# Two-block transformer on one core: filler and convolution taps of the differential stage dealt by what each part costs

## The chip, the cores and the metric

The program runs on one core of one Trainium2 chip. The metric is the device time of one execution in microseconds. The kernel before took 3533.0 us in the median of three runs (3526.06 to 3537.19). TensorE (PE) multiplies matrices, VectorE (DVE) and ScalarE (ACT) work on rows of 128 partitions, GpSimd (POOL) likewise, SyncE (SP) issues the transfers.

## What is computed

Two transformer blocks, one behind the other, over 1024 rows of 1024 columns, all in fp32. The change lies in the second block, in its differential attention and its depthwise convolution:

```
h = rms_norm(x, attn_norm_w)
q, k, v, u, g = split(h @ w_in)                 # 1024, 1024, 1024, 2048, 2048 columns
q, k = rms_norm(q), rms_norm(k)                 # over 64 columns, 8 heads x 2 maps
p = softmax(q1 k1' * scale + bias, causal) - lam * softmax(q2 k2' * scale + bias, causal)
a = rms_norm(p @ v) ...                         # per head, over 128 columns
c = conv31(u_a * sigmoid(u_b))                  # causal, depthwise, 31 taps, 1024 channels
x = x + (g_a * (a @ w_proj_attn) + g_b * (silu(layer_norm(c)) @ w_proj_conv)) @ w_out
x = x + (silu(h2 @ w_gate) * (h2 @ w_up)) @ w_down
```

## The kernel before

fp32 products are made of three passes: each operand is split into a rounded high part and a remainder (`_hi`, `_lo`), and hi x hi, lo x hi and hi x lo are added up in PSUM. ScalarE rounds a tile of weights (`ring.round`, line 171), GpSimd subtracts (`ring.subtract`, line 179), through a ring of two slots; SyncE loads them.

The stage is `differential_and_conv`. Its attention runs in 64 steps: head h = s // 8, query block b = s % 8 of 128 rows, with (b + 1) x 128 keys. A step has three parts, x = 0, 1, 2; all engines walk the same list of steps and parts, each in its own queue, and wait on semaphores. In step s:

- TensorE: `score(s)` for both maps into `sc` (line 2471), then the parts. In each part it does its share of the *filler*: the projections of the next head's q, k, b, a, v tiles and of gate tiles G, 48 matmuls of 512 columns a tile in two halves of 24 (line 197). In part 0 of every odd step also `values` for a pair of earlier steps (line 2492), and in parts 0 and 2 `turn_t`, the transposes of the probabilities of step s - 1 into the one `bank` (line 341). `turn_t` waits for `mixed` (GpSimd) and for `t_low` of the block before it; `values` waits for the `t_low` of its own blocks.
- VectorE: `top(s)` adds the bias and takes the negated maximum (lines 2340, 2344); then in each part the first share of its convolution taps, in part 0 `weights` (2349, 2351), in parts 0 and 2 `low_t` (2358), the remainder of the turned block; then what the part has of `feed_conv` (2293), `low_v`, `normalise`, `low_q`, `low_k`; then the second share of the taps. A tap (2272) multiplies 128 x 1024 of the padded input by one weight per channel and adds to `acc`.
- ScalarE: `expose(s)`, both exponentials (2162), needs `top(s)`; then in each part, in this order: a square of a norm (2119), `take` of the projected halves that end in this part, each second half with the rounding of the weights two tiles on and, for b, with a table load, the sigmoid and a table load (2101 to 2104); `round_t` in parts 0 and 2 (2178); `weigh` in part 0 (2170); `copy_out`, `round_v`, `invert` (2126, 2129), `round_q`, `round_k`.
- GpSimd: weight subtractions, and in part 0 `mix(s)` (2056), which adds the two weighted maps.

Which part of a head has the extra work of a norm is set by constants: V_TURN = 4, Q_SQUARE = 5, O_SQUARE = 6, K_SQUARE = 8 (a part is numbered 3b + x, 0 to 23). The square is taken at that part, the sum of squares and the division one part later (q: in the same part), the rounding of k two parts later.

The filler was dealt over the steps by fixed weights (13, 13, 13, 13, 12, 12, 11, 11) and evenly over the three parts. The 31 taps of a head (13 of head 0 come before the loop) were dealt over the parts between the end of this head's `feed_conv` and two parts before the next one, so that TAP = 1.45 us a tap plus an estimate of VectorE's other work in each part follows an estimate of TensorE's (`pe_load`, `dve_load`).

Of the kernel before, what the change touches and what calls it, by code (L numbers as in the profile page):

```python
# [1851 lines left out]
def differential_and_conv(nc, ring, w_in, h_hi, h_lo, bias_rows, lam, ones, eps, qk_gain, subln, conv_w, conv_b,  # L1852
# [6 lines left out]
    with ExitStack() as stack:  # L1859
# [81 lines left out]
        def pe_load(at):  # L1941

            s, x = divmod(at, PARTS)
            b = s % QB
            lo, hi = part(s, x)
            return 0.231 * (hi - lo) + (0.24 * (b + 1) if x == 0 else 0.44) + (0.72 * (b + 1) if x == 0 and b % 2 else 0)

        def dve_load(at):

            s, x = divmod(at, PARTS)  # L1950
            b = s % QB
            load = {V_TURN: 1.4, Q_SQUARE: 1.3, Q_SQUARE + 1: 2.7, O_SQUARE + 1: 1.6, K_SQUARE + 1: 1.3,
                    K_SQUARE + 2: 2.6}.get(b * PARTS + x, 0)
# [301 lines left out]
        def _(dve):  # L2255
# [619 lines left out]
```

## Time and profile before

| | |
|---|---|
| median of three runs | 3533.0 us |
| the profiled execution | 3531.41 us, its span 3529.6 us |
| mean granted clock of TensorE | 0.919 |
| busy: PE, DVE, ACT, POOL | 3006.8, 1612.5, 1256.4, 711.3 us |
| taps (line 2272) | 240, 397.2 us, 1655 ns each |
| filler of the stage (line 197, d_pp) | 3 x 896 matmuls, 368.0, 368.8 and 366.0 us |

The stage's steps lie between about 1408 and 2286 us of the span. Head 0 starts at 1408 on TensorE, and the five heads after it take some 110 us each up to head 4; heads 5 and 6 have seven tiles of filler instead of six. Busy time of matmuls counts their overlapping ends: their pitch is shorter than their mean duration (0.233 us against some 0.4).

### The profile page before, as it was taken

To read this page: it belongs to the slowest core of one execution; us is meant where nothing else is said; L and a number is where in the kernel's file an instruction comes from. 1 tells how busy PE (TensorE), PEld (TensorE's weight loads), DVE (VectorE), ACT (ScalarE), POOL (GpSimd) and SP (SyncE) were. 2 spreads that over 40 slices of the span, in tenths; PEclk is the share of its full clock that TensorE was granted. 3 is DMA by queue.
4 is the path that set the end of the run, shared out by engine and by line. 5 is a ranking of instruction groups with operands and counts; after the bars stand their busy time and mean duration, and the time that the engine had idled before them with its cause. 6 is when DMAs were issued, how large, how long until landed. Compare 5 with 4: busy or idle time off the path is not lost. (4 is left out here: it accounts for less than half of the span.)

```text
span 3529.6 us, 35907 instructions
## 1 busy us (share of the span) xinstructions
PE 3006.8 (85%) x13416; PEld 2422.7 (69%) x13416; DVE 1612.5 (46%) x1983; ACT 1256.4 (36%) x2003; POOL 711.3 (20%) x317
## 2 busy tenths in 40 slices
PE   6999998766668859989889899977686998998998
PEld 5787886555556747767767677754475787787786
DVE  3665651356654333777877787511432221111121
ACT  3555541344442143555555445432223111111110
POOL 2111111100002211323332233211312121121211
PEclk8999999888869979999999999988798999999999
DMA  4111222000004312121221112133230111111112
GB/s 111 38 54 48 66 67 59 18 8 7 9 0 146 111 66 63 48 61 38 62 60 50 55 51 75 69 137 107 95 125 18 48 48 42 42 48 42 42 48 72
DMA packets 232494, 207.77 MB, mean 59 GB/s; under 512 B 25224, under 2 KB 196776, under 8 KB 232360
## 3 DMA queue, kind: packets, MB, share of 16 engines
q1 hardware_dynamic: 231328, 204.40, 18.6%
q10 hardware_dynamic: 1032, 1.57, 0.3%
q8 instruction: 85, 1.39, 0.2%
q14 instruction: 49, 0.40, 0.0%
HBM read 156.13 MB, written 41.42 MB: 56 GB/s over the span
## 5 line engine op out<-in xcount | busy, mean ns | idle before, releaser
L179 POOL TENSOR_TENSOR w_lo<-w_raw,w_hi 128x1024 fp32r<-128x1024 f32 (+2 forms) x228 | 536.5, 2355 | 2214.7 <-ACT w_hi L171 2214.7
L171 ACT ACTIVATE w_hi<-w_raw 128x1024 fp32r<-128x1024 f32 (+2 forms) x228 | 223.7, 985 | 780.1 <-PE u_y_ps L1649 222.4
L2272 DVE SCALAR_TENSOR_TENSOR d_acc<-d_padded,vectors,d_acc 128x1024 f32<-128x1024 f32 x240 | 397.2, 1655 | 4.5
L197 PE MATMUL d_pp<-h_hi,w_hi 128*128 128x512 f32 x896 | 368.0, 411 | 12.2 <-PEq L67 5.2
L197 PE MATMUL d_pp<-h_hi,w_lo 128*128 128x512 f32 x896 | 368.8, 412 | 0.0
L197 PE MATMUL d_pp<-h_lo,w_hi 128*128 128x512 f32 x896 | 366.0, 408 | 0.0
L197 PE MATMUL s_pp<-h_hi,w_hi 128*128 128x512 f32 x512 | 206.8, 404 | 12.1 <-PEq L67 12.1
L197 PEld LDWEIGHTS d_pp<-h_hi,w_hi 128*128 128x128 f32 x896 | 175.1, 195 | 56.0 <-issue 18.0
L2056 POOL TENSOR_TENSOR d_probs<-d_probs 128x128 f32<-128x128 f32 (+3 forms) x64 | 123.5, 1930 | 410.4 <-ACT d_probs L2170 410.2
L197 PE MATMUL s_pp<-h_hi,w_lo 128*128 128x512 f32 x512 | 205.2, 401 | 0.0
L197 PE MATMUL s_pp<-h_lo,w_hi 128*128 128x512 f32 x512 | 204.2, 399 | 0.0
L197 PEld LDWEIGHTS d_pp<-h_lo,w_hi 128*128 128x128 f32 x896 | 174.3, 195 | 41.8 <-issue 2.6
L197 PEld LDWEIGHTS d_pp<-h_hi,w_lo 128*128 128x128 f32 x896 | 174.9, 195 | 39.8 <-issue 2.1
L2162 ACT ACTIVATE d_probs<-d_sc,d_stats 128x256 f32<-128x256 f32 (+7 forms) x128 | 94.3, 739 | 295.5 <-DVE d_stats L2344 295.0
L1649 PE MATMUL u_y_ps<-w_hi,ff_hi 128*128 128x512 f32 x352 | 140.7, 400 | 27.1 <-PEq L67 27.1
L1649 PE MATMUL u_y_ps<-w_hi,ff_lo 128*128 128x512 f32 x352 | 140.1, 398 | 0.0
L1649 PE MATMUL u_y_ps<-w_lo,ff_hi 128*128 128x512 f32 x352 | 139.5, 396 | 0.0
L1633 DVE TENSOR_TENSOR x_tok<-u_y_ps,x_tok 128x512 f32<-128x512 f32 x48 | 33.2, 691 | 232.4 <-PE u_y_ps L1649 232.4
L227 PE MATMUL t_g<-h_hi,w_hi 128*128 128x512 f32 x352 | 114.0, 406 | 15.2 <-DVEq L208 15.2
L197 PEld LDWEIGHTS s_pp<-h_hi,w_hi 128*128 128x128 f32 x512 | 97.3, 190 | 31.9 <-issue 12.4
L2680 DVE TENSOR_TENSOR t_t<-t_g,t_t 128x1024 f32<-128x1024 f32 x22 | 26.9, 1225 | 197.0 <-ACT t_t L2660 197.0
L2683 DVE TENSOR_TENSOR t_t<-t_u,t_t 128x1024 f32<-128x1024 f32 x22 | 26.9, 1224 | 195.8 <-PE t_u L227 195.8
(320 smaller groups left out, 6621.0 us busy)
## 6 DMA issues: line engine op xcount, KB each, us to landing
w_raw<-in_w_in SPq DMA_DIRECT2D x97, 512.0 KB, 4.0
w_raw<-in_w_gate_up SPq DMA_DIRECT2D x44, 512.0 KB, 3.9
w_raw<-in_w_down SPq DMA_DIRECT2D x22, 512.0 KB, 3.8
gates<-s_gate SPq DMA_DIRECT2D x16, 512.0 KB, 5.2
f_gate<-gates SPq DMA_DIRECT2D x16, 512.0 KB, 4.8
w_raw<-in_w_out SPq DMA_DIRECT2D x16, 512.0 KB, 4.1
w_raw<-in_w_proj SPq DMA_DIRECT2D x16, 512.0 KB, 5.0
x_tok_in<-in_x SPq DMA_DIRECT2D x8, 512.0 KB, 8.5
```

The source lines that it names most:

```text
L171: act.activation(self.hi[:, s, 0:chunks, :], self.raw[:, s, 0:chunks, :], ACT.Copy).then_inc(self.rounded[s], 1)
L179: pool.tensor_tensor(self.lo[:, s, 0:chunks, :], self.raw[:, s, 0:chunks, :], f32(self.hi[:, s, 0:chunks, :]), ALU.subtract).then_inc(self ...
L197: mm = pe.matmul(halves(ps)[h], w[:, k, :], x[:, k, h * HALF:(h + 1) * HALF], start=(k == 0 and r == 0), stop=(k == chunks - 1 and r == 2))
L227: mm = pe.matmul(halves(ps)[h], w[:, k, :], x[:, k, h * HALF:(h + 1) * HALF], start=(k == 0 and r < 2), stop=(k == chunks - 1 and r > 3))
L1633: dve.tensor_tensor(x, y_ps[b][:, :], x, ALU.add).then_inc(added, 1)
L1649: mm = pe.matmul(y_ps[b][:, :], y[:, k, b * P:(b + 1) * P], ww[:, i * HALF:(i + 1) * HALF], start=(k == 0 and r == 0), stop=(k == chunks - ...
L2056: pool.tensor_tensor(probs[:, s % 2, 0:n], probs[:, s % 2, 0:n], probs[:, 2, 0:n], ALU.add).then_inc(c["mixed"], 1)
L2162: act.activation(probs[:, slot, 0:n], sc[:, a, 0:n], ACT.Exp, bias=st[:, 1:2], accum_out=st[:, 2:3]).then_inc(c["prob"], 1)
L2272: dve.scalar_tensor_tensor(out=acc[:, :], in0=x, scalar=wt, in1=acc[:, :], op0=ALU.mult, op1=ALU.add).then_inc(c["taps"], 1)
L2680: dve.tensor_tensor(t[:, s, :], g_ps[s][:, :], t[:, s, :], ALU.mult).then_inc(silu[s], 1)
L2683: dve.tensor_tensor(t[:, s, :], u_ps[s][:, :], t[:, s, :], ALU.mult).then_inc(product[s], 1)
```

## The change

The first hunk deals the filler. `pe_work(h, at)` gives the microseconds that TensorE has in a part apart from filler; each part gets filler up to one common level of the head, so that filler (0.231 us a matmul) and the rest make equal sums, and a part above the level gets none. K_SQUARE moves from 8 to 9.

The second deals the taps. `dve_work(at)` gives VectorE's other microseconds in a part; each part of a head's room gets taps in proportion to what the level (all work of the room over its parts) leaves there, at least 0.2. TAP is 1.65. The room ends one part ahead of the next head's first `feed_conv` instead of two. The third halves a part's taps around the part's other work, and in part 0 of a step an odd tap comes first.

```diff
-        weight = [13, 13, 13, 13, 12, 12, 11, 11]
+        V_TURN, Q_SQUARE, O_SQUARE, K_SQUARE = 4, 5, 6, 9
+        def pe_work(h, at):
+            b, x = divmod(at, PARTS)
+            turned = min(4, b) if b else 4
+            work = {V_TURN: 0.9, Q_SQUARE: 1.7 * (h < LAST), O_SQUARE + 1: 1.7 * (h > 0),
+                    K_SQUARE + 1: 1.7 * (h < LAST)}.get(at, 0)
+            if x == 0:
+                work += 0.23 * (b + 1) + 0.11 * turned + {1: 2.9, 3: 0.7, 5: 1.5, 7: 2.2}.get(b, 0)
+            if x == 2:
+                work += 0.11 * (max(b - 4, 0) if b else 4)
+            return work
...
-            total = each[h] * SIX
-            at = [base + total * sum(weight[:b]) // sum(weight) for b in range(QB + 1)]
-            base += total
-            ends += [[lo + (hi - lo) * x // PARTS for x in range(PARTS + 1)] for lo, hi in zip(at, at[1:])]
+            fixed = [pe_work(h, at) for at in range(PARTS * QB)]
+            room = 0.231 * each[h] * SIX
...
+            total, share = 0.0, [max(level - f, 0) for f in fixed]
+            at = [base]
+            for x in share:
+                total += x
+                at.append(base + round(each[h] * SIX * total / sum(share)))
...
-        conv_end = [part_of[stream.index(("a", h)), 0] - 2 for h in range(1, HEADS)] + [PARTS * (STEPS - 1)]
+        conv_end = [part_of[stream.index(("a", h)), 0] - 1 for h in range(1, HEADS)] + [PARTS * (STEPS - 1) + 1]
-        TAP = 1.45
+        TAP = 1.65
...
+            n = CONV - (TAPS_FIRST if h == 0 else 0)
+            level = (sum(dve_work(at) for at in room) + TAP * n) / len(room)
+            free = [max(level - dve_work(at), 0.2) for at in room]
+            total, done = 0.0, 0
+            for at, x in zip(room, free):
+                total += x
+                upto = n if at == room[-1] else round(n * total / sum(free))
...
-            def taps(at, lo, hi):
+            def taps(at, first_half):
...
-                    for t in range(x + (y - x) * lo // 4, x + (y - x) * hi // 4):
+                    middle = x + (y - x + (at % PARTS == 0)) // 2
+                    for t in range(x, middle) if first_half else range(middle, y):
                         tap(h, t)
```

Worked out from these lines for head 2 (heads 1 to 4 are alike but for a tap), the steps separated by bars, the three parts of a step in a group:

```
filler before  12 13 13 | 12 13 13 | 12 13 13 | 12 13 13 | 12 12 12 | 11 12 12 | 10 11 11 | 11 11 11
filler after   14 16 15 |  1 13  9 | 12 10 16 |  8  9 17 |  9 17 16 |  2 17 16 |  7 17 15 |  0 17 15
taps before     0  3  2 |  1  2  1 |  0  0  2 |  2  0  3 |  0  0  0 |  0  2  2 |  0  1  2 |  4  2  2
taps after      0  3  2 |  1  1  2 |  0  2  2 |  1  1  1 |  1  2  0 |  0  0  2 |  0  3  2 |  0  2  3
```

The halves of a tile end, before, in parts 1 and 3 (q), 5 and 7 (k), 9 and 11 (b), 13 and 15 (a), 17 and 19 (v), 21 and 23 (G); after, in parts 1 and 4, 6 and 8, 10 and 12, 14 and 16, 17 and 19, 22 and 23. Taps of heads 0 to 7, before: 33, 31, 31, 31, 31, 34, 26, 18; after: 30, 31, 31, 31, 31, 35, 25, 21.

## Rows read from the trace of the kernel before

**Rows 1.** Busy by window: length, PE, PEld, DVE, ACT, POOL, then clock, DMA, GB/s
```profile
1628.00:1739.00 111.00, 98.78 (x453) 79.09 (x452) 85.23 (x95) 59.91 (x101) 32.67 (x14) 0.93 0.18 54
1964.00:2087.50 123.50, 111.21 (x504) 88.45 (x503) 96.76 (x98) 61.48 (x104) 35.11 (x15) 0.96 0.19 56
2087.50:2199.00 111.50, 107.58 (x505) 85.96 (x504) 77.69 (x92) 61.59 (x104) 34.43 (x15) 0.99 0.20 60
2193.00:2286.00 93.00, 90.89 (x450) 74.50 (x448) 61.80 (x75) 45.46 (x88) 24.80 (x14) 1.00 0.20 69
```

**Rows 2.** Waits of TensorE, 1628 to 1739 us: total, times, longest
```profile
PE d_bank L341 <- DVE d_t_lo L2358: 6.7, 1, 6.7
PE d_sc L2471 <- ACT d_probs L2162: 4.4, 1, 4.4
```

**Rows 3.** Windows as in rows 1, before and behind the longer hole
```profile
1585.30:1619.80 34.50, 34.50 (x176) 28.69 (x175) 27.92 (x29) 19.79 (x33) 13.19 (x5) 1.00 0.15 46
1622.90:1633.00 10.10, 5.63 (x16) 4.60 (x17) 9.33 (x13) 2.09 (x7) 2.92 (x2) 0.50 0.18 54
```

**Rows 4.** Waits of VectorE, 1628 to 1739 us: total, times, longest
```profile
DVE d_stats L2349 <- ACT d_probs L2162: 7.7, 6, 2.2
DVE d_t_lo L2358 <- ACT d_t_hi L2178: 6.1, 7, 1.4
DVE d_raw L2305 <- ACT d_probs L2129: 5.8, 2, 2.9
DVE d_o_sb L2305 <- ACT d_probs L2129: 2.6, 1, 2.6
DVE d_q L2311 <- ACT d_q L2136: 1.5, 1, 1.5
DVE d_sc L2340 <- PE d_sc L2471: 0.5, 1, 0.5
```

**Rows 5.** Timeline of VectorE, one head: start, duration, ..., [idle before <- releaser]
```profile
1616.24 10.52 DVE L2272 SCALAR_TENSOR_TENSOR d_acc<-d_padded,vectors,d_acc 128x1024 f32<-128x1024 f32 x5
...
1637.77 0.69 DVE L2358 TENSOR_TENSOR d_t_lo<-d_bank,d_t_hi 128x512 fp32r<-128x512 f32 x1 [1.35 <-ACT d_t_hi L2178]
...
1643.65 0.29 DVE L2358 TENSOR_TENSOR d_t_lo<-d_bank,d_t_hi 128x128 fp32r<-128x128 f32 x1 [1.35 <-ACT d_t_hi L2178]
...
1653.81 1.29 DVE L2305 SCALAR_TENSOR_TENSOR d_raw<-d_raw,vectors,d_probs 128x1024 f32<-128x1024 f32 x1 [2.90 <-ACT d_probs L2129]
...
1667.10 1.29 DVE L2305 SCALAR_TENSOR_TENSOR d_o_sb<-d_o_sb,d_gain,d_probs 128x1024 f32<-128x1024 f32 x1 [2.57 <-ACT d_probs L2129]
...
1678.21 1.28 DVE L2305 SCALAR_TENSOR_TENSOR d_raw<-d_raw,vectors,d_probs 128x1024 f32<-128x1024 f32 x1 [2.91 <-ACT d_probs L2129]
...
1692.94 0.17 DVE L2349 RECIPROCAL d_stats<-d_stats 128x2 f32<-128x2 f32 x1 [1.73 <-ACT d_probs L2162]
```

**Rows 6.** Timeline of ScalarE: a taken half with a weight rounding, two table loads
```profile
1641.75 0.59 ACT L2097 ACTIVATE d_raw<-d_pp 128x512 f32<-128x512 f32 x1
1642.22 1.05 ACT L171 ACTIVATE w_hi<-w_raw 128x1024 fp32r<-128x1024 f32 x1
...
1683.40 1.28 ACT L2101 ACT_TABLE_LOAD   x1
...
1685.78 1.28 ACT L2104 ACT_TABLE_LOAD   x1
```

**Rows 7.** Timeline of VectorE, head 5, step 3
```profile
2018.43 0.56 DVE L2358 TENSOR_TENSOR d_t_lo<-d_bank,d_t_hi 128x384 fp32r<-128x384 f32 x1 [4.94 <-ACT d_t_hi L2178]
```

**Rows 8.** Instructions of tile d_acc: ns shortest/median/longest
```profile
L2272 DVE SCALAR_TENSOR_TENSOR d_acc<-d_padded,vectors,d_acc x240: 1267/1285/3311, 1360.8 to 2284.4; 128x1024 f32<-128x1024 f32 x120
```

**Rows 9.** Costliest groups of the page: busy us, mean ns, idle before
```profile
L2272 DVE SCALAR_TENSOR_TENSOR d_acc<-d_padded,vectors,d_acc 128x1024 f32<-128x1024 f32 x240 | 397.2, 1655 | 4.5
```

**Rows 10.** Timeline of GpSimd: mixing of step 7, a weight subtraction
```profile
1617.76 3.32 POOL L2056 TENSOR_TENSOR d_probs<-d_probs 128x1024 f32<-128x1024 f32 x1 [6.15 <-ACT d_probs L2170]
...
1664.90 2.41 POOL L179 TENSOR_TENSOR w_lo<-w_raw,w_hi 128x1024 fp32r<-128x1024 f32 x1 [2.74 <-ACT w_hi L171]
```

More of the change, by code:

```diff
@@ L1907, in differential_and_conv @@
         TILES = len(stream)
-        weight = [13, 13, 13, 13, 12, 12, 11, 11]
+        V_TURN, Q_SQUARE, O_SQUARE, K_SQUARE = 4, 5, 6, 9
[9 more added lines that the diff above has]
+            return work
         ends, base = [], 0
         for h in range(HEADS):
-            total = each[h] * SIX
-            at = [base + total * sum(weight[:b]) // sum(weight) for b in range(QB + 1)]
-            base += total
-            ends += [[lo + (hi - lo) * x // PARTS for x in range(PARTS + 1)] for lo, hi in zip(at, at[1:])]
+            fixed = [pe_work(h, at) for at in range(PARTS * QB)]
+            room = 0.231 * each[h] * SIX
+            level = 0.0
+            for lower in sorted(fixed):
+                under = [f for f in fixed if f <= lower]
+                if sum(lower - f for f in under) <= room:
+                    level = (room + sum(under)) / len(under)
+            total, share = 0.0, [max(level - f, 0) for f in fixed]
[3 more added lines that the diff above has]
+                at.append(base + round(each[h] * SIX * total / sum(share)))
+            base += each[h] * SIX
+            ends += [at[PARTS * b:PARTS * (b + 1) + 1] for b in range(QB)]
         def part(s, x):
@@ L1936, in differential_and_conv, with dve_work @@
         conv_in_at = [-1] + [part_of[stream.index(("a", h)), 1] for h in range(1, HEADS)]
-        conv_end = [part_of[stream.index(("a", h)), 0] - 2 for h in range(1, HEADS)] + [PARTS * (STEPS - 1)]
+        conv_end = [part_of[stream.index(("a", h)), 0] - 1 for h in range(1, HEADS)] + [PARTS * (STEPS - 1) + 1]
         TAPS_FIRST = 13
-        TAP = 1.45
-        def pe_load(at):
+        TAP = 1.65
+        def dve_work(at):
             s, x = divmod(at, PARTS)
[L1944 to L1953, printed above, removed]
-            load += sum(0.7 for t, e in halves_in(s, x) if stream[t][0] == "a")
-            return load + (1.7 + 0.27 * (b + 1) + 0.4 if x == 0 else 0.5 if x == 2 and b > 4 else 0)
-        V_TURN, Q_SQUARE, O_SQUARE, K_SQUARE = 4, 5, 6, 8
+            h, b = divmod(s, QB)
+            load = {V_TURN: 1.4, Q_SQUARE: 1.3, Q_SQUARE + 1: 2.7, O_SQUARE + 1: 1.3, K_SQUARE + 1: 1.3,
+                    K_SQUARE + 2: 2.5}.get(at % (PARTS * QB), 0) * (h < LAST or at % (PARTS * QB) in (V_TURN, O_SQUARE + 1))
+            load += sum(0.7 for t, e in halves_in(s, x) if stream[t][0] == "a")
+            if x == 0:
+                load += 0.5 + (1.15 + 0.28 * (b + 1) if b < 4 else 0.8 + 0.285 * (b + 1))
+                load += 0.15 + 0.135 * (min(4, b) if b else 4)
+            if x == 2 and (b == 0 or b > 4):
+                load += 0.15 + 0.135 * (b - 4 if b else 4)
+            return load
         taps_in = {}
@@ L2378, in _ @@
                     at = b * PARTS + x
-                    taps(PARTS * s + x, 0, 2)
+                    taps(PARTS * s + x, True)
                     if s < STEPS and x == 0:
@@ L2400, in _ @@
                         low_k(h + 1)
-                    taps(PARTS * s + x, 2, 4)
+                    taps(PARTS * s + x, False)
             normalise("o", LAST)
```

6 lines of the change are left out of this document (removed).

## The prediction

> **What bounds the kernel now.** I read the busy windows first, one for each head of the stage. A head of the middle of the stage (heads 1 to 4) takes 111 us; in it TensorE (PE) is busy 98.8 us at a mean clock of 0.93, VectorE (DVE) 85.2 us [rows 1]. By these shares TensorE seems to set the pace and to have 12 us of holes. The waits say who made them: 6.7 us for VectorE's rounding remainder of the turned block (`low_t`) and 4.4 us for ScalarE's exponential [rows 2]. Each is one wait per head, and behind each the clock falls: behind the longer one 10.1 us pass at 0.50, that is at 1.2 GHz, while the 34.5 us of unbroken work before it ran at 1.00 [rows 3]. A mean of 0.93 over the head [rows 1] is 0.14 x 111 = 15.5 us at half clock, and costs half of it. So a head without the two would be 111 - 11.1 - 7.8 = about 92 us on TensorE.
>
> The waits of VectorE are the view that decides. In the same head they sum to 24.2 us: 7.7 + 6.1 + 5.8 + 2.6 + 1.5 + 0.5 [rows 4]. 85.2 + 24.2 = 109.4 of 111 us. VectorE is either working or standing for a short round trip over ScalarE, practically never for TensorE alone (0.5 us for the scores). So VectorE's in-order chain, work plus round trips, is the pace of heads 1 to 4, and TensorE's two large holes are only where that lag is collected. Over heads 0 to 5 the same holds (head 5: 96.8 us busy of 123.5); head 6 has 77.7 busy of 111.5 and head 7 61.8 of 93, where TensorE is 91 busy [rows 1]: there TensorE sets the pace, in head 7 wholly.
>
> **What that makes of the change.** Filler, scores and taps are the same in number. Levelling removes the places where the lag is collected, not the lag. A head gets shorter only by what VectorE's round trips lose, by taps that leave heads 0 to 5, and by what taps lose less to GpSimd. I count these for heads 1 to 4, part by part (part 3b + x is the x-th of step b, 0 to 23 in a head), on VectorE's queue.
>
> Round trips that shrink. (a) Part 3: a lone tap now stands between `top` and `weights` and covers that wait, one of the short ones among the six that make 7.7, about 0.6 [rows 4]; `q`'s second half is no longer taken in this part (with a weight rounding of 1.05), so the `low_t` wait of 1.35 goes: -2.0 [rows 5, 6]. (b) Part 2: the wait of 1.35 is for TensorE's transposes; a lagging VectorE doesn't meet it: -1.35 [rows 5]. (c) `normalise("q")` in part 5 waited 2.90; one tap now stands ahead of it: about -1.9 [rows 5]. (d) `normalise("o")` in part 7 waited 2.57; the taking of `k` with its weight rounding (0.59 + 1.05) leaves ScalarE's queue in front of it and one tap stands ahead: -2.6 [rows 5, 6]. (e) Part 12: the lone tap covers 1.2 of the 1.73 in front of `weights` [rows 5]. (f) The weight rounding leaves part 15, as in part 3: -1.4; the small rest of the `low_t` waits and the score wait, -1.3 [rows 4]. Sum -11.7.
>
> Round trips that grow. (g) The second half of `b` now ends in part 12, the first of a step. There ScalarE takes it before it rounds the turned block: 0.6 for the half, 1.05 for the next weights, then table, sigmoid and table, 3.66 from the first load's start to the second's end, 5.3 in all [rows 6], and `low_t` stands behind it on VectorE. In head 5 this order exists already and that one wait is 4.94 us [rows 7]. In heads 1 to 4 the old order has it in part 11, where nothing waits. +5.4. (h) Part 4 has one tap, behind `low_v`; in front stood two. After `weights` ScalarE has the scaling, 0.59, 1.05 and a half of v to do, some 3.1, VectorE only a `low_t` of 0.3: wait about +2.8 (estimate from [rows 6]). (i) Keys one part later: the square now stands behind `expose` of step 3 and in front of its rounding: `low_t` +0.9, and `normalise("k")` has 0.6 of `b` more before it: 2.91 becomes 3.7, +0.8 [rows 5, 6]. (j) Part 6: the taking of `k` stands before the rounding: +0.5. (k) Part 21 had four taps, two of them between `top` and `weights`; it has none, so the longest wait of that kind, 2.2, is met: +2.2 [rows 4]. In parts 15 and 18 nothing changes: no tap there before, none now. Sum +12.6.
>
> Net +0.9 us a head, nothing that the levelling was to win. Its bounds: if (c), (h) and (k) fall half as favourably, +6; if VectorE's lag hides (h) and (i), -5.
>
> **Taps beside GpSimd.** A tap alone takes 1.27, the longest 3.31 [rows 8], the mean is 1.655 [rows 9]. Five taps beside a mixing of 3.32 took 10.52, where alone they would be 6.35 [rows 5, 10]; a weight subtraction is 2.41 where no tap runs [rows 10]. 31 taps x 0.385 = 12 us of a head go to this. Spread taps meet more of GpSimd's 32.7 us [rows 1], (g) makes a wait in which GpSimd works alone. From -2 to +3 a head; I take +0.5. The Trainium skill (GPSIMD Engine Reference, Key points) says that GpSimd shares its SBUF interfaces with VectorE and contends with its instructions of two SBUF inputs, which a tap is; by that rule a levelled deal has no cheaper place for taps, and the trace agrees (1.27 against up to 3.31).
>
> **(g) by the skill.** The Trainium skill (ScalarE: Activation LUTs, What ACT_TABLE_LOAD costs) gives a switch of tables about 2.66 us, load and drain. Two of them with the sigmoid would be 6.4 us and (g) 2.7 larger, some +11 us over heads 1 to 4. The trace shows both loads and the sigmoid in 3.66 us with no such drain, so the trace is used.
>
> **The other heads.** Head 0 gets 30 taps instead of 33: 3 x 1.6 = -4.9, with +1 for round trips -4 (0 to -8). Head 5 has one tap more (+1.6) and shorter trips in parts 3 and 6, since the weight roundings leave first parts (-3.2), but loses the covers in parts 15 and 21 (+2.4) and has `b`'s sigmoid in front of `normalise("k")` instead of `low_t` (-0.6): 0, from -4 to +6. Head 6, 25 taps for 26, at last partly TensorE's: -2, from -8 to +3. Head 7 is TensorE's: 21 taps for 18 stand beside it, but parts 3 and 21 have filler of 1 and 0, so `values` meets the remainder of a block turned just ahead (a rounding and a remainder of some 0.6 each and their hand-overs, against 0.7 of score and filler; an estimate): 1 to 2 us each: +2, from 0 to +4.
>
> What TensorE loses is beside this. It will wait in part 10 for the squared keys (4 to 6 us, behind `top` of step 3), in part 3 for `low_t` (up to 4), in part 21 (2 to 3): three holes instead of two (estimates from the queue positions above), each likely followed by a stretch at half clock, as in [rows 3]. They cost nothing as long as VectorE is later; if that cover is gone a stretch costs half its length, 3 to 5 us, up to once a head. SP's queue: the convolution store and the key copies fall behind the same weight tiles as before, nothing is delayed. The four edits of the tap costs (1.65, `dve_work`, the halving, 22 parts) are worth nothing by themselves beyond the places counted.
>
> **Sum.** Heads 1 to 4: 4 x (0.9 + 0.5) = +6; head 0 -4; head 5 0; head 6 -2; head 7 +2: +2. Profiled execution 3531.4, of which 3529.6 is the span: 3533.4. The median of the runs, 3533.0, is 1.6 above the profiled one: **3535**.
>
> **Rivals.** (1) *Levelled, so TensorE's pace.* If VectorE's round trips were mostly caused by its lag, both engines would run through and heads 1 to 4 fall to some 91 to 93 us, head 5 to 108: 4 x 19 + 15 + 12 for heads 0 and 6 = about -100: 3433. For it: 12 us of holes and the half clock. Against: 24.2 us of waits stand on VectorE's own queue and only 0.5 + 1.35 of them have TensorE as cause [rows 4, 5]. 7%. (2) *Half of it.* (h), (i), (k) hidden, the wins stand, taps dodge GpSimd: -5 to -7 a head in heads 1 to 4, -4 in head 0: about -22 to -30, 3508. 22%. (3) *Slower: TensorE becomes late for VectorE at part 4.* The wait in part 3 (filler 1 where 12 stood) costs it up to 4 us and then the half clock; `turn_v` follows within a part, `low_v` waits for it, then `normalise("q")` for its sums. It decides from the point where TensorE leaves `values` less than one part ahead of VectorE's `top`. Price 3 to 6 us a head over heads 1 to 5: +15 to +30, with the sum above about 3557. For it: a hole of only a few us was followed by the half clock each time [rows 3]; against: VectorE's lag of 5 to 10 us at this place. 29%. (4) *It doesn't do what it says*: the parts are equal by TensorE's unhindered costs, and the engine isn't unhindered; this is my forecast, no change: 42%, its own range 3523 to 3544.
>
> Within 0.3% (10.6 us) this kernel can't be told from no change. Faster 0.29 (rivals 1 and 2), same 0.42, slower 0.29. The range for 8 in 10 leaves out rival 1 and the end of rival 3: 3503 to 3562.
>
> **What would show it.** Right: heads 1 to 4 still 109 to 114 us, VectorE's busy time plus waits over 98% of it; one `low_t` wait of about 5 us per head in step 4; `normalise("k")` waiting over 3.5; TensorE's long wait now at the sum of squares of k (line 2445) instead of the score; the clock in the stage still 0.92 to 0.95. Wrong: heads of 100 us or less, or VectorE waiting for TensorE's scores or turned blocks, or waits of a head that sum to under 18 us.

## The result, and the profile after

The changed kernel took 3568.64 us in the median of four runs (3563.39 to 3572.45), the kernel before 3535.1 (3526.06 to 3537.73) beside it: ratio 1.0098 with the interval [1.0074, 1.0123]. It is 34 us slower. The forecast was no change (3535) with 3562 as the upper end of its range, so it was wrong. The profiled execution took 3565.79 us, 34.4 more than the one of before.

The windows of the changed kernel, one for each of heads 0, 2, 5, 6 and 7, cut at TensorE's first score of a head; the columns are those of [rows 1].

```profile
1408.90:1515.40 106.50, 91.55 (x416) 72.52 (x415) 76.66 (x87) 54.48 (x92) 30.57 (x14) 0.95 0.19 55
1631.70:1747.80 116.10, 101.05 (x455) 79.16 (x454) 85.50 (x95) 59.43 (x102) 32.10 (x15) 0.94 0.17 51
1976.10:2103.70 127.60, 112.96 (x502) 88.89 (x500) 99.12 (x100) 62.77 (x107) 37.35 (x16) 0.93 0.19 57
2103.70:2223.50 119.80, 109.81 (x502) 86.75 (x501) 77.08 (x90) 61.56 (x104) 31.32 (x15) 0.96 0.19 58
2223.50:2316.00 92.50, 84.43 (x411) 68.77 (x410) 60.25 (x72) 39.95 (x79) 25.93 (x13) 0.96 0.20 67
```

From the first score of one head to that of the next, TensorE takes (us; head 7 up to the first score of its last step):

| head | 0 | 1 | 2 | 3 | 4 | 5 | 6 | 7 |
|---|---|---|---|---|---|---|---|---|
| before | 98.2 | 109.9 | 111.8 | 110.0 | 114.1 | 127.1 | 114.0 | 79.6 |
| after | 106.5 | 116.3 | 116.1 | 116.0 | 112.3 | 127.6 | 119.8 | 88.3 |

The sum is 38.2 us more: 8.3 in head 0, 14.9 in heads 1 to 4, 0.5 in head 5, 5.8 in head 6, 8.7 in head 7. Outside the stage some 4 us go the other way. Counted from VectorE's own first `top` of one head to that of the next, head 0 goes from 109.0 to 112.6 us, heads 1 to 4 from 446.0 to 462.7, head 5 from 123.4 to 124.4 and head 6 from 111.2 to 119.4: together the same, but for head 0 only +3.6. The rest of TensorE's +8.3 is lead that it lost: VectorE's first `top` of head 1 came 11.3 us behind TensorE's first score of it, and comes 6.5 us behind it now.

The waits of VectorE in head 2 of the changed kernel (total, times, longest), which answer to [rows 4]:

```profile
DVE d_t_lo L2379 <- ACT d_t_hi L2198: 9.2, 5, 5.3
DVE d_stats L2370 <- ACT d_probs L2182: 8.3, 6, 2.4
DVE d_raw L2326 <- ACT d_probs L2149: 6.1, 2, 4.6
DVE d_v_lo L2345 <- ACT d_v_hi L2170: 3.6, 1, 3.6
DVE d_q L2332 <- ACT d_q L2156: 1.5, 1, 1.5
```

They sum to 28.7, where before they were 24.2. With 85.5 us of work that is 114.2 of the 116.1 us. The wait for `o`'s norm (2.6 before) has gone, the one for `low_v` is new, and the longest `low_t` wait is 5.3 instead of 1.4. TensorE's waits in the same window, which answer to [rows 2]:

```profile
PE d_o_ps L2513 <- DVE d_t_lo L2379: 7.3, 2, 5.0
PE d_sc L2466 <- ACT d_probs L2139: 6.0, 2, 4.1
PE d_o_ps L2513 <- ACT d_o_sb L2207: 1.6, 1, 1.6
```

They sum to 14.9 us, where the same head of before has 12.6. The row of the taps on the page, which answers to [rows 9]: 1631 ns each instead of 1655.

```profile
L2292 DVE SCALAR_TENSOR_TENSOR d_acc<-d_padded,vectors,d_acc 128x1024 f32<-128x1024 f32 x240 | 391.5, 1631 | 4.2
```

### The profile page after: what moved, and what is told of

It is laid out like the page before. It is cut to its first block and busy times, and to the rows that moved or that the text cites. A ratio compares the mean times of both kernels' runs of the same rounds, so it can differ in the third digit from the quotient of the medians.

```text
span 3564.0 us, 35907 instructions
## 1 busy us (share of the span) xinstructions
PE 3017.3 (85%) x13416; PEld 2418.2 (68%) x13416; DVE 1605.5 (45%) x1983; ACT 1254.4 (35%) x2003; POOL 705.2 (20%) x317
## 5 line engine op out<-in xcount | busy, mean ns | idle before, releaser
L2292 DVE SCALAR_TENSOR_TENSOR d_acc<-d_padded,vectors,d_acc 128x1024 f32<-128x1024 f32 x240 | 391.5, 1631 | 4.2
L2076 POOL TENSOR_TENSOR d_probs<-d_probs 128x128 f32<-128x128 f32 (+3 forms) x64 | 113.3, 1770 | 538.3 <-ACT d_probs L2190 538.3
L227 PE MATMUL t_g<-h_hi,w_hi 128*128 128x512 f32 x352 | 113.8, 405 | 15.2 <-DVEq L208 15.2
L197 PEld LDWEIGHTS s_pp<-h_hi,w_hi 128*128 128x128 f32 x512 | 97.0, 190 | 32.2 <-issue 12.6
```

What stands on the lines that cost most here:

```text
L197: mm = pe.matmul(halves(ps)[h], w[:, k, :], x[:, k, h * HALF:(h + 1) * HALF], start=(k == 0 and r == 0), stop=(k == chunks - 1 and r == 2))
L227: mm = pe.matmul(halves(ps)[h], w[:, k, :], x[:, k, h * HALF:(h + 1) * HALF], start=(k == 0 and r < 2), stop=(k == chunks - 1 and r > 3))
L2076: pool.tensor_tensor(probs[:, s % 2, 0:n], probs[:, s % 2, 0:n], probs[:, 2, 0:n], ALU.add).then_inc(c["mixed"], 1)
L2292: dve.scalar_tensor_tensor(out=acc[:, :], in0=x, scalar=wt, in1=acc[:, :], op0=ALU.mult, op1=ALU.add).then_inc(c["taps"], 1)
```

## Experiments

Each was timed beside the kernel before, whose median was 3532 to 3534 us in each group; ratios are against it. The changed kernel's own ratio is 1.0098 [1.0074, 1.0123]; a run whose interval overlaps this one can't be told from the changed kernel by its time alone. The head lengths of one trace are steadier: where an edit touches only the last head, heads 0 to 6 came out the same within 0.1 us (`gate_first`, below). "Heads 1 to 4" is the mean of their lengths on TensorE: 111.5 before, 115.2 after.

### The two halves of the change

`fill_only` is the kernel before with the new deal of filler and K_SQUARE = 9. `taps_only` is the changed kernel with the old deal of filler:

```diff
 # taps_only, against the changed kernel
-        V_TURN, Q_SQUARE, O_SQUARE, K_SQUARE = 4, 5, 6, 9
+        V_TURN, Q_SQUARE, O_SQUARE, K_SQUARE = 4, 5, 6, 8
+        weight = [13, 13, 13, 13, 12, 12, 11, 11]
         ends, base = [], 0
         for h in range(HEADS):
-            fixed = [pe_work(h, at) for at in range(PARTS * QB)]
...
-            ends += [at[PARTS * b:PARTS * (b + 1) + 1] for b in range(QB)]
+            total = each[h] * SIX
+            at = [base + total * sum(weight[:b]) // sum(weight) for b in range(QB + 1)]
+            base += total
+            ends += [[lo + (hi - lo) * x // PARTS for x in range(PARTS + 1)] for lo, hi in zip(at, at[1:])]
```

> The kernel before with the new deal of filler and K_SQUARE = 9, but the old deal of taps (old costs, old room, old halving). Theory A (VectorE's in-order chain of work and round trips over ScalarE is the pace; the new filler moves ScalarE's long jobs into first parts): the filler carries the whole loss, heads 1 to 4 take 116 to 118 us, the kernel 3565 to 3578 us. Rival B (TensorE's holes and the half clock behind them are the loss, levelled filler alone lessens them): 3535 to 3550. Rival C (the taps stand in the wrong parts): about 3535.

> The changed kernel with the old deal of filler and K_SQUARE = 8: only the taps are dealt the new way. Theory A: round trips of a head change by less than 1 us and heads 0 to 5 lose three taps: 3530 to 3540 us, as before. Rival C (the taps carry the loss): 3555 or more. Rival B: two long holes of TensorE a head as before, 3535.

Measured: `fill_only` 3584.05 (1.0144 [1.0123, 1.0166]), `taps_only` 3570.65 (1.0116 [1.0092, 1.0140]). Either half loses by itself, and together they lose no more than the smaller: 3568. Both theories that put the loss into one half fell; `fill_only` is also 6 us over the range of its theory A. In head 2 of both the length is 117.1 us, and VectorE's work and waits are 84.6 + 30.8 and 87.4 + 28.1. Some of the waits are the same in both halves and stand only once in the whole change: the new one for `low_v` is 2.7 us in `fill_only`, 3.6 in `taps_only` and 3.6 in the changed kernel.

### Two orders on ScalarE's queue

```diff
 # k_square_early
-                    if h < LAST and at == K_SQUARE:
-                        square_of("k", h + 1)
 # behind the takings of the part
+                    if h < LAST and at == K_SQUARE - 1:
+                        square_of("k", h + 1)
 # turned_first, ahead of the takings
+                    u = s - 1
+                    if x == 0 and 0 <= u < STEPS:
+                        round_t(u, 0)
...
-                    u = s - 1
-                    if x in (0, 2) and 0 <= u < STEPS and x // 2 < CHUNKS[u % QB]:
+                    if x == 2 and 0 <= u < STEPS and x // 2 < CHUNKS[u % QB]:
                         round_t(u, x // 2)
```

> The changed kernel with the square of k taken by ScalarE at the end of part 8 instead of at the start of part 9, so that it no longer stands behind the exponentials of step 3; nothing else moves. TensorE's wait for the squared k (4.1 us a head, with a stretch of half clock) must go. Theory A: VectorE gains only the rounding in front of low_t (0.65) and the late logarithm in normalise(k) (about 0.9), 1.5 us a head, 7 heads: -10 us, 3558. Rival B (TensorE's holes cost what they last): -5 to -6 us a head, -35 to -40 us, 3530.

> The changed kernel with ScalarE rounding the turned block before it takes a projected half in the first part of a step (round_t ahead of take, so ahead of the weight rounding and the sigmoid with its two table loads too). Theory A: the low_t wait of 5.3 us in step 4 of heads 0 to 4 falls under 0.7, some 0.5 elsewhere: -6 us a head, 5 heads, -30 us: 3540. Rival B: TensorE's holes are elsewhere (k, values): under -8 us, 3562. Rival D (GpSimd: its weight subtraction no longer runs beside an idle VectorE): half of the gain is lost to slower taps, 3553.

> The changed kernel with two orders on ScalarE's queue altered together: the square of the next k at the end of part 8 (alone 6 us faster than the changed kernel), and the rounding of the turned block ahead of the taking of b in parts 3b (alone 6 us slower, though the wait of 5.3 us that it was to remove went). Theory A' (coupled chains): the second edit alone removed a wait of VectorE in step 4 and met it again in step 5, because TensorE stood 5 us for the sum of squares of k; with the square early that hole is smaller, so the wait of 5.3 stays removed: 3540 to 3552, heads 1 to 4 at 111 to 113 us. Rival B' (each order only has its own price, added up): 3568 - 6 + 6 = about 3568. Rival C (the loss lies in the places of taps and filler and no order can give it back): 3558 to 3565.

Measured: `k_square_early` 3562.78 (1.0086 [1.0062, 1.0110]), `turned_first` 3574.39 (1.0126 [1.0102, 1.0150]), `both_orders` 3560.84 (1.0075 [1.0058, 1.0093]). All three intervals overlap that of the changed kernel. `k_square_early` lies 5 us over theory A's 3558 and far from B's 3530, and its heads 1 to 4 take 113.8; `turned_first` lies over all three of its values. It took the 5.30 us away from `low_t` in step 4, but one part-17 wait of the same kind grew from 1.22 to 4.42, in the timeline of VectorE:

```profile
1721.65 0.29 DVE L2381 TENSOR_TENSOR d_t_lo<-d_bank,d_t_hi 128x128 fp32r<-128x128 f32 x1 [4.42 <-ACT d_t_hi L2198]
```

Its head 2 stayed at 116.0, and head 6 grew from 119.8 to 124.6. Both together gave 113.4 there with `low_t` waits of 5.9 in sum, but head 1 and 3 stayed at 115.4 and 115.3, and the time is not to be told from that of `k_square_early` alone, outside what coupling foretold (3540 to 3552) and inside the range of the case in which no order gives the loss back. So one hand-over removed can be met again; this left open whether any wait of VectorE comes off one for one.

### Which engine's chain: one engine relieved

In the tiny pair 30 of a head's 31 taps work on 128 of 1024 columns; in the thin pair 46 of the 48 matmuls of a tile of filler have 128 of 512 columns. Both leave out work and keep every instruction and its order.

```diff
 # tiny
-                    dve.scalar_tensor_tensor(out=acc[:, :], in0=x, scalar=wt, in1=acc[:, :], op0=ALU.mult,
+                    dve.scalar_tensor_tensor(out=acc[:, 0:P], in0=x[:, 0:P], scalar=wt, in1=acc[:, 0:P], op0=ALU.mult,
 # thin
+        n = HALF if thin is None or i % half == 0 else thin
-        mm = pe.matmul(halves(ps)[h], w[:, k, :], x[:, k, h * HALF:(h + 1) * HALF],
+        mm = pe.matmul(halves(ps)[h][:, 0:n], w[:, k, :], x[:, k, h * HALF:h * HALF + n],
```

> The kernel before with 30 of the 31 taps of each head working on 128 of their 1024 columns (work left out, the order of all instructions kept). VectorE's busy time falls by about 30 x 1.3 = 39 us a head, to some 46. Theory A (VectorE's chain is the pace of heads 0 to 5): heads 1 to 4 fall from 111 us to TensorE's own pace; that is 98.8 of work at clock 0.93, some 91 to 97, so 8 heads give -100 to -130 us: 3400 to 3435. Rival B (TensorE's holes come of the deal of filler, not of VectorE's lateness): heads stay above 103 us, 3470 to 3500.

> The changed kernel with 30 of the 31 taps of each head working on 128 of their 1024 columns (work left out, order kept). Theory A (the loss is in VectorE's chain of work and waits): with VectorE early the levelled filler is as good as the old or better, 0 to 15 us below the same edit of the kernel before. Rival B (the new places of the filler and of k's square hole TensorE by themselves): still 20 to 35 us slower than the same edit of the kernel before, with heads 1 to 4 at 3 to 5 us more.

> tiny_after (the changed kernel, 30 of 31 taps of a head on 128 columns) with ScalarE's square of the next k at the end of part 8. In tiny_after TensorE's waits of a head are 4.7 us for squares, 1.6 for o's rounding, 0.7 for a remainder, beside none in tiny_before. Theory D (the new filler leaves too little TensorE work ahead of the sum of squares of k): the wait of 2.9 us goes, heads 1 to 4 fall from 100.5 to 96.5 to 98 us, time 3455 to 3466 against 3475. Rival (another ScalarE job is then late): 3470 to 3478.

> The kernel before with the filler of the stage made thin: of each tile's 48 matmuls the first of each half keeps its 512 columns, the other 46 do 128 (work left out, all order kept). TensorE falls from 94 us a head to under 50, so VectorE's chain is alone. Theory D (two separate prices: the new filler costs TensorE 6 us a head, as with tiny taps 94.1 against 100.3; the new taps cost VectorE's chain another): heads 1 to 4 at 103 to 109 us, since VectorE's 85 busy and 24 of waits stay; time 3460 to 3510. Rival A'' (VectorE's waits are mostly TensorE's lateness): heads under 98 us, below 3440.

> The changed kernel with the same thin filler (work left out, order kept). Theory D: the new taps cost VectorE's own chain 3 to 7 us a head without any lateness of TensorE, so 20 to 45 us slower than thin_before. Rival E (the new taps are fine and cost only where they meet TensorE's stretches): within 10 us of thin_before, then TensorE's 6 us is the whole price and the coupling passes it on.

| | before | after | after less before |
|---|---|---|---|
| as it is | 3535.1 | 3568.6 | 34 |
| tiny taps | 3422.1 | 3475.0 | 53 |
| thin filler | 3525.9 | 3571.9 | 46 |
| heads 1 to 4, tiny taps | 94.1 | 100.6 | 6.5 |
| heads 1 to 4, thin filler | 111.9 | 115.8 | 3.9 |

Windows of one head with tiny taps, before and after:

```profile
1683.80:1777.90 94.10, 93.88 (x456) 75.33 (x454) 56.32 (x95) 59.80 (x102) 26.39 (x15) 1.00 0.22 64
```

```profile
1712.00:1812.40 100.40, 95.64 (x455) 76.05 (x453) 52.97 (x94) 59.51 (x102) 25.95 (x15) 0.98 0.20 59
```

With VectorE relieved the old filler keeps TensorE 93.88 of 94.10 us busy at clock 1.00: nothing is left to level. The new filler opens holes, which was rival B of `tiny_after`; at 53 us and 6.5 us a head they cost more than it said (20 to 35 and 3 to 5). TensorE's waits of that one head, after:

```profile
PE d_sc L2466 <- ACT d_probs L2139: 3.8, 2, 2.9
PE d_o_ps L2513 <- DVE d_t_lo L2379: 0.7, 1, 0.7
PE d_o_ps L2513 <- ACT d_o_sb L2207: 0.3, 1, 0.3
```

4.8 us, against 0.2 before, and the clock of 0.98 stands for most of the other 1.6. Equal sums per part take the filler out of the parts with most other work (1 matmul in part 3, 2 in part 15, 0 in part 21). Of the waits, 0.7 stands in part 3 and 0.3 in part 15, as if the filler there had covered them; the longest, 2.9, stands in part 10, behind the square of k that moved to part 9, where 8 matmuls of filler stand instead of 12. `tiny_after_k_early` took 3469.48, with heads 2 to 4 at 99.4 instead of 100.5; the expectation was 96.5 to 98 and 3455 to 3466. The wait of 2.9 did go, but in its head 3 a new one of 2.1 us, in step 4 for the bank that the taking of `b` frees, came for it, so moving the square gives back only about 1 us of the 6.

Windows of one head with thin filler, before and after:

```profile
1629.60:1740.90 111.30, 82.23 (x456) 73.45 (x454) 85.81 (x95) 59.24 (x102) 32.51 (x14) 0.75 0.18 54
```

```profile
1632.30:1748.30 116.00, 81.26 (x455) 71.59 (x454) 86.13 (x95) 59.22 (x102) 32.72 (x14) 0.76 0.17 52
```

Some 72% of the filler's columns are gone (46/48 x 3/4), TensorE is granted 0.75 of its clock, and the heads are as long as with all of it: 111.3 (111.8 before) and 116.0 (116.1). TensorE's busy time fell less than the expectation had it (82.2 us, not under 50), but it is 17 us less than in the whole kernel, and its idle time of the head rose from 12.6 to 29.1 us. The heads of `thin_before` came out over both of its cases (103 to 109, and under 98); rival E of `thin_after` fell, and theory D's 20 to 45 us stand against 46, of which 16 lie in heads 1 to 4 and 14 in head 7. VectorE's waits in the thin changed kernel are nearly those of the whole one (28.1 and 28.7 us in sum):

```profile
DVE d_t_lo L2380 <- ACT d_t_hi L2199: 10.0, 5, 5.3
DVE d_stats L2371 <- ACT d_probs L2183: 8.3, 6, 2.4
...
```

This shows that in the middle heads of both kernels VectorE's chain, its work with the round trips over ScalarE, is the pace, and that it carries the difference there without TensorE's filler (3.9 us a head here, 3.7 in the whole kernels). No run makes ScalarE's own work light, so how much of the round trips is its queue and how much the hand-overs is open. The pair doesn't explain why the halves of the change don't add up: TensorE's chain of 100.6 us is far under the 115.2 of the heads, and either half loses on VectorE's chain.

It also shows what can't tell which engine is the pace. In the kernel before, head 2, TensorE's busy time and waits are 99.2 + 12.6 of 111.8 us, as full a sum as VectorE's 86.0 + 24.2. With tiny taps, where TensorE is the pace, VectorE's are still 56.3 + 36.2 of 94.1, or 98%, and again nearly all for ScalarE:

```profile
DVE d_t_lo L2358 <- ACT d_t_hi L2178: 11.2, 8, 2.7
DVE d_stats L2349 <- ACT d_probs L2162: 10.0, 8, 2.2
DVE d_raw L2305 <- ACT d_probs L2129: 7.7, 2, 4.8
...
```

So neither a full sum nor the name in the releaser's column decides; the light pairs do.

### The last head's gate store

```diff
 # gate_first: the load-ahead behind the store, on SyncE's queue
-                if t == TILES:
-                    ring.load_ahead(sp)
...
                     store_gate(stream[at][1])
+                if t == TILES:
+                    ring.load_ahead(sp)
```

> The changed kernel with one DMA order altered: the gate store of the last head (b's sigmoid) is issued ahead of the load-ahead of the output projection's weights on SP's queue. Theory A: head 7's hole of 7.1 us on TensorE (VectorE's wait of 8.4 us for the first remainder of the projection stage) goes, nothing else moves: heads 0 to 6 unchanged, time 3558 to 3564 against 3568. Rival: the weight loads then come later and the hole turns into a wait for w_raw of the same size: 3566 to 3570.

> The kernel before with the two edits of order that stand apart from the deal: ScalarE rounds the first turned block of a step ahead of the taking of a projected half (parts 3b), and SyncE issues the last head's gate store ahead of the load-ahead of the projection's weights. Theory: head 7's hole of 5.5 us goes (it gave 8 to 10 us in the changed kernel), head 5 loses its remainder wait of 4.94 us, heads 1 to 4 move by -2 to +1: 3515 to 3526 against 3534. Rival (what is taken from one wait is met at the next, as with turned_first): only the gate's 5 us: 3527 to 3531.

Measured: `gate_first` 3558.63 (1.0072 [1.0053, 1.0091]), head 7 at 80.0 instead of 88.3, all others within 0.1, and a time inside the expectation. The two intervals of the times overlap; the trace of head 7 decides. The reason stands in the changed kernel's timeline of SyncE (the load-ahead waits 23.34 us for its ring slots, the gate store is behind it) and of ScalarE, whose taking of the next gate half waits for that store's buffer, with VectorE's `low_t` behind it:

```profile
2273.10 23.34 SPq L160 DMA_DIRECT2D w_raw<-in_w_proj  x2
2296.49 5.84 SPq L2025 DMA_DIRECT2D gate_b<-d_sig  x3
```

```profile
2301.37 0.60 ACT L2104 ACTIVATE d_sig<-d_pp 128x512 f32<-128x512 f32 x1 [9.16 <-issue]
```

```profile
2302.17 0.29 DVE L2379 TENSOR_TENSOR d_t_lo<-d_bank,d_t_hi 128x128 fp32r<-128x128 f32 x1 [8.40 <-ACT d_t_hi L2198]
```

`before_two_orders`, the same edit and `turned_first` on the kernel before, took 3539.86 (1.0014 [0.9998, 1.0031]): nothing gained, and over both cases of its expectation. Head 5 fell by 3.3, less than its wait of 4.94, but head 6 rose by 2.9, heads 1 to 4 by 1.6 in the mean, and head 7 fell by only 1.3. There the hole was ScalarE's alone: in the kernel before its taking of the same half waited 5.46 us for the gate store, but the remainder behind it on VectorE, which TensorE needs, waited 0.71:

```profile
2265.51 0.29 DVE L2358 TENSOR_TENSOR d_t_lo<-d_bank,d_t_hi 128x128 fp32r<-128x128 f32 x1 [0.71 <-ACT d_t_hi L2178]
```

### Do covered waits come off the time?

`norms_last` moves, in the kernel before, the second share of a part's taps ahead of the division by the norm and of `low_q` and `low_k`; `after_norms_last` does so in the changed one. `taps_by_waits` adds a deal by hand in heads 1 to 4, same 20 parts, same 31 taps (ahead of the part's other work, behind it):

```diff
+        BY_WAITS = [(1, 0), (1, 1), (1, 0), (1, 0), (0, 1), (2, 0), (0, 1), (2, 0), (0, 1), (2, 0), (0, 1), (0, 1),
+                    (0, 0), (0, 0), (0, 0), (0, 0), (1, 1), (1, 1), (2, 0), (0, 1), (1, 1), (2, 1), (1, 1), (1, 0)]
                         low_v(h)
+                    taps(PARTS * s + x, 2, 4)
                     if h < LAST and at == Q_SQUARE:
                         normalise("q", h + 1)
```

> The kernel before with one order on VectorE changed: in every part the second share of its taps stands ahead of the division by the norm and of low_q and low_k instead of behind them (in heads 1 to 4 one tap each in parts 5 and 9, none in 7). Theory D (VectorE's chain of work and round trips alone is the pace; each wait that a tap covers shortens the head by that wait): the two waits of 2.90 and 2.91 us shrink by a tap of 1.3 to 1.6 each, heads 1 to 4 at 108 to 109.5 instead of 111.4, all heads 0 to 5 about -3 each: 3512 to 3522 against 3533. Rival F (what is taken from one wait is met at the next, as with the rounding ahead of the taking): 3530 to 3536.

> norms_last, and in heads 1 to 4 the 31 taps dealt by hand over the same 20 parts so that a tap or two stand right ahead of each long wait of VectorE (two ahead of the division of q, of o and of k, two and two between top and weights in parts 18 and 21, one in parts 0, 2, 3, 12's rest unchanged), old filler. Theory D: waits of a head fall from 24 to about 12 us, heads 1 to 4 from 111 to 100 to 104 us: 3480 to 3505. Rival F: TensorE's own round trips (values behind low_t) are pushed late and heads stay at 108 or more: 3515 or more.

> The changed kernel with the same order edit as norms_last (in heads 1 to 4 the second shares of parts 4, 5, 8 and 10: one tap each, of part 6 and 9 none or one). Theory D: the wait of low_v is left, the waits for the divided q (1.57) and k (4.57) shrink by a tap of 1.3 to 1.6 each: heads 1 to 4 at 113 us, 3550 to 3558 against 3568. Rival F: 3562 to 3570.

> taps_by_waits, and the last head's gate store issued ahead of the load-ahead of the projection's weights on SyncE's queue. By gate_first in the changed kernel, where it gave 8 to 10 us, of which the hole was 7.1, the hole of 5.5 us should go: 3 to 7 us below taps_by_waits. By before_two_orders, where head 7 moved by only 1.3: within 2 us of it.

| | time | ratio | head 2 | VectorE's work + waits |
|---|---|---|---|---|
| norms_last | 3526.14 | 0.9982 [0.9971, 0.9992] | 109.7 | 86.1 + 21.9 |
| taps_by_waits | 3506.51 | 0.9929 [0.9908, 0.9949] | 105.7 | 83.6 + 20.7 |
| taps_by_waits_gate | 3507.42 | 0.9928 [0.9907, 0.9948] | 105.8 | |
| after_norms_last | 3557.45 | 1.0066 [1.0045, 1.0087] | 114.9 | 86.6 + 26.6 |

In `norms_last` the two waits of 2.90 and 2.91 became 1.59 and 1.72, as a tap of 1.3 would have it, but 1.13 of the second came back as a new wait for `low_k`:

```profile
1648.49 1.28 DVE L2305 SCALAR_TENSOR_TENSOR d_raw<-d_raw,vectors,d_probs 128x1024 f32<-128x1024 f32 x1 [1.59 <-ACT d_probs L2129]
...
1671.71 1.28 DVE L2305 SCALAR_TENSOR_TENSOR d_raw<-d_raw,vectors,d_probs 128x1024 f32<-128x1024 f32 x1 [1.72 <-ACT d_probs L2129]
1674.13 2.47 DVE L2318 TENSOR_TENSOR d_k_lo<-d_raw,d_k_hi 64x1024 fp32r<-64x1024 f32 x2 [1.13 <-ACT d_k_hi L2144]
```

The time, 0.18% lower, lies between the two expectations, and so do heads 1 to 4 (110.4). `after_norms_last` agrees with theory D: heads 1 to 4 at 113.2 in the mean, 3557. `taps_by_waits` is faster beyond doubt, 27 us below the kernel before and 62 below the changed one, with the old deal of filler. Its waits of VectorE and its window, head 2:

```profile
1609.60:1715.30 105.70, 96.25 (x454) 76.44 (x453) 83.58 (x95) 59.92 (x102) 31.95 (x14) 0.97 0.19 57
```

```profile
DVE d_t_lo L2369 <- ACT d_t_hi L2188: 7.5, 6, 2.5
DVE d_stats L2360 <- ACT d_probs L2172: 4.9, 3, 2.2
DVE d_raw L2316 <- ACT d_probs L2139: 4.4, 2, 3.2
DVE d_v_lo L2335 <- ACT d_v_hi L2160: 3.6, 1, 3.6
DVE d_q L2322 <- ACT d_q L2146: 0.3, 1, 0.3
```

The waits of `o`'s norm (2.57) and the `stats` waits of parts 0, 3 and 18 (3.3 in sum) did go, and the norm of q fell from 2.90 to 1.18. But `low_t` rose from 1.35 to 2.50 in part 2 and to 2.08 in part 3, `low_v` waits 3.6 where it had none, and the norm of k waits 3.2 though both taps of its part stand ahead of it, in front of `weights`. The waits fell to 20.7, not to 12: a wait that is covered comes off in part, and part is met later. Of the 6.1 us of head 2, 3.5 are waits and 2.4 are work (86.0 before in this head); 2.1 of the work are the 30 multiply-and-add taps, 46.9 us instead of 49.0, of which 11 instead of 12 overlap work of GpSimd. The time is 1.5 us over the upper end of the expectation, and heads 1 to 4 with 106.2 in the mean are over its 104. The gate store's place is worth nothing here: 3507.42, as the rival had it.

## Why the prediction was wrong, by its own steps

**What bounds the kernel: right, but not by the argument given.** I took 85.2 + 24.2 = 109.4 of 111 us for the proof. By the tiny pair such a sum, and the small share of TensorE among the releasers, is also found where TensorE is the pace (92.5 of 94.1). What shows VectorE's chain as the pace of the middle heads is the thin pair.

**The sum over the heads.** On TensorE's windows the forecast was +2 and +38.2 came. The difference is 12.3 us in head 0, 8.9 in heads 1 to 4, 7.8 in head 6, 6.7 in head 7 and 0.5 in head 5. The steps that failed, in this order, are the round trips of head 0, put at +1 instead of +9.1; the sum of those of heads 1 to 4, put at +0.9 a head instead of +4.5 in head 2; what TensorE loses in head 6, put at nothing; and the queue of SyncE in head 7, put at nothing instead of 8.3.

**The round trips of heads 1 to 4: the mechanism right, the sum mis-sized.** The timeline of VectorE in the changed kernel's head 2, long waits only:

```profile
1651.85 0.29 DVE L2379 TENSOR_TENSOR d_t_lo<-d_bank,d_t_hi 128x128 fp32r<-128x128 f32 x1 [0.78 <-ACT d_t_hi L2198]
1655.71 1.29 DVE L2345 TENSOR_TENSOR d_v_lo<-d_sc,d_v_hi 128x512 fp32r<-128x512 f32 x2 [3.57 <-ACT d_v_hi L2170]
1661.09 1.28 DVE L2326 SCALAR_TENSOR_TENSOR d_raw<-d_raw,vectors,d_probs 128x1024 f32<-128x1024 f32 x1 [1.57 <-ACT d_probs L2149]
...
1667.88 0.42 DVE L2379 TENSOR_TENSOR d_t_lo<-d_bank,d_t_hi 128x256 fp32r<-128x256 f32 x1 [1.29 <-ACT d_t_hi L2198]
...
1684.95 0.56 DVE L2379 TENSOR_TENSOR d_t_lo<-d_bank,d_t_hi 128x384 fp32r<-128x384 f32 x1 [0.65 <-ACT d_t_hi L2198]
1690.08 1.28 DVE L2326 SCALAR_TENSOR_TENSOR d_raw<-d_raw,vectors,d_probs 128x1024 f32<-128x1024 f32 x1 [4.57 <-ACT d_probs L2149]
1700.15 0.17 DVE L2370 RECIPROCAL d_stats<-d_stats 128x2 f32<-128x2 f32 x1 [0.54 <-ACT d_probs L2182]
1705.87 0.69 DVE L2379 TENSOR_TENSOR d_t_lo<-d_bank,d_t_hi 128x512 fp32r<-128x512 f32 x1 [5.30 <-ACT d_t_hi L2198]
...
1719.27 0.29 DVE L2379 TENSOR_TENSOR d_t_lo<-d_bank,d_t_hi 128x128 fp32r<-128x128 f32 x1 [1.22 <-ACT d_t_hi L2198]
...
1742.54 0.17 DVE L2370 RECIPROCAL d_stats<-d_stats 128x2 f32<-128x2 f32 x1 [2.37 <-ACT d_probs L2182]
```

| step | forecast | measured |
|---|---|---|
| (a) part 3 | -2.0 | -1.2 (`low_t` kept 0.78) |
| (b) part 2 | -1.35 | -1.35 |
| (c) norm of q | -1.9 | -1.33 |
| (d) norm of o | -2.6 | -2.57 |
| (e) part 12 | -1.2 | -1.19 |
| (f) part 15 and small ones | -2.7 | -2.9 |
| (g) sigmoid ahead of `low_t` | +5.4 | +5.30 |
| (h) `low_v` | +2.8 | +3.57 |
| (i) keys later | +1.7 | +2.1 |
| (j) part 6 | +0.5 | +0.49 |
| (k) part 21 | +2.2 | +2.37 |
| `low_t` in part 17 | none | +1.22 |
| sum | +0.9 | +4.5 |

All eleven steps are within 0.8 us, and the largest term, (g), within 0.1. The sum is off by 3.6 because every miss of more than 0.2 us, one wait left out among them, fell on one side. The +4.5 lies between the sum and its upper bound of +6. Head 2 is not the worst: VectorE's waits grew by 6.1 and 5.9 us in heads 1 and 3, and by 3.2 in head 4. Heads 1 to 4 measured +14.9, where +6 stood in the sum with the contention. For (g), an estimate from the 2.66 us that the Trainium skill (ScalarE: Activation LUTs, What ACT_TABLE_LOAD costs) gives for each switch would have made the term 2.7 larger; the wait of 5.30 decides for the durations of [rows 6].

**Contention with GpSimd** was forecast at +0.5 a head. In head 2 the 30 multiply-and-add taps took 49.0 us in both kernels, so it was nothing there; over the whole stage a tap became 24 ns cheaper, not dearer.

**Head 0, forecast -4, measured +8.3.** This is the worst step. I let taps leave and gave the round trips +1. The taps did leave: on VectorE's own steps of head 0, before and after, its work fell by 5.5 us, where the term was -4.9.

```profile
1409.10:1518.20 109.10, 94.75 (x434) 75.97 (x434) 88.76 (x94) 56.37 (x96) 35.85 (x15) 0.95 0.20 60
1409.40:1522.00 112.60, 97.65 (x445) 77.53 (x445) 83.21 (x91) 56.40 (x96) 34.13 (x15) 0.95 0.19 55
```

What failed are the round trips. Its longest waits are the same as in the middle heads:

```profile
DVE d_t_lo L2379 <- ACT d_t_hi L2198: 9.6, 4, 5.3
DVE d_stats L2370 <- ACT d_probs L2182: 8.9, 5, 2.4
DVE d_sc L2361 <- PE d_sc L2492: 6.8, 2, 5.9
DVE d_raw L2326 <- ACT d_probs L2149: 5.3, 2, 4.3
...
```

With two of 1.5 each they sum to 33.6, where head 0 of before has 24.5: +9.1 against +1. Terms (g), (h), (i) and (k) belonged into head 0 too. By these two terms VectorE's head 0 is 3.6 us longer; the other 4.7 of the 8.3 are the lead that TensorE no longer has at its end.

**Head 6, forecast -2, measured +5.8.** TensorE sets the pace here, as the prediction said of this head, and then "They cost nothing as long as VectorE is later" does not hold. With tiny taps head 6 goes from 106.1 to 113.1, so the new filler costs TensorE 7.0 here with VectorE's taps nearly out of the way; one wait for the bank that `feed_conv` empties grows from 0.8 to 3.7. Between the whole kernels it grows from 1.5 to 4.7:

```profile
PE d_sc L2466 <- ACT d_probs L2139: 4.8, 2, 3.8
PE d_pp L197 <- DVE d_padded L2314: 4.7, 1, 4.7
```

**Head 7, forecast +2, measured +8.7.** Of SP's queue it said "nothing is delayed"; this was false, and `gate_first` gives 8.3 of it back. I had not followed the last gate store past the load-ahead.

**Head 5: forecast 0, measured +0.5.** The size is right, but no run shows its terms one by one, and the halves of the change move this head by +7.6 (`fill_only`) and -2.4 (`taps_only`), so that the balance near zero is in part luck.

**The rivals.** The third (slower, 3557, at 29%) had the direction, but not for its reason alone: its place, TensorE late for VectorE at part 4, is seen (`low_v` waits 3.57), at less than 1 us over what (h) already held. The first, TensorE's pace if all is levelled, fell: that pace, 94.1 us in the tiny kernel before (my estimate was 92), was open to the old filler and the new one makes it 100.6.

**The signs named in advance.** One 5 us `low_t` wait in step 4, over 3.5 for the norm of k, and a clock near 0.94 all came; heads of 109 to 114 did not, except head 4 (112.3). TensorE's wait for the sum of squares of k came (4.1 us in head 2), but its longest is one of 5.0 for `low_t` at `values`. Work plus waits over 98% of the head came too (114.2 of 116.1), and by the tiny pair it would have come with either engine as the pace.

**What stays open.** Why the two halves together lose less than either price added up, but for the wait of `low_v`. How much of `fill_only`'s loss is K_SQUARE and how much the deal itself, and which hand-overs, besides the square of k (about 1 us net), make up the 6.5 us a head that the new filler costs TensorE: the rows name three waits, and none but the square's was removed by itself.

## What to carry to other kernels

Where an in-order engine's work and short waits fill its time, place movable work by what waits there, not by how much else the part holds: levelling loads took cover from the round trips on both engines at once, while taps put ahead of the waits gave 0.7%. An in-order engine's work and waits fill its time whoever is the pace, so make each engine in turn light, with its order kept, in both versions; that shows which chain sets the time and what the change costs on each. Cut each engine's windows at its own steps: an engine that lags by 11 us has that much of a head's work in the next window. And when a sum is made of ten small terms of both signs, count every head and every queue with them, since a difference of a few us is what is left over.

## What the runs showed of the hardware

Thinning 46 of 48 filler matmuls lowered TensorE's granted clock in the head from 0.92 to 0.75 (by its two levels, half of the head at 1.2 GHz), and the head was no longer for it. With tiny taps the engine was unbroken and the clock 1.00. In head 2 of the changed kernel TensorE idled five times, for 2.3, 1.9, 4.1, 1.6 and 5.0 us; behind all but the fourth it was granted 0.50 for some 3.4 us. The prediction had a hole followed by the half clock each time. In `tiny_after` head 3 has a hole of 2.9 us with such a stretch behind it, and head 2 has the same hole, and three shorter ones, at 1.00 throughout:

```profile
1611.80:1711.90 100.10, 94.02 (x455) 75.20 (x454) 52.97 (x94) 59.43 (x102) 25.96 (x15) 1.00 0.20 60
```

Of the 228 multiply-and-add taps of the stage's loop in the kernel before, the 134 that overlap no work of GpSimd took 1.28 us and never more than 1.29; the 94 that do took 2.22 in the mean and up to 3.31. VectorE's work in head 2, with the same 31 taps, is from 83.6 (`taps_by_waits`) to 87.4 us (`taps_only`), 2.6 of the difference in the 30 multiply-and-add taps. The Trainium skill (GPSIMD Engine Reference, Key points) says that GpSimd contends with VectorE's instructions of two SBUF inputs; the runs agree and give its size here, up to 3.8 us a head by the places of the taps, which I had thought to be about the same for any spread deal.
